# Feed-forward matmuls that stream their moving columns, and write their PSUM columns, last first

## The chip, the core and the metric

The kernel runs on one core of one Trainium2 chip. Its time is the device time of one execution in microseconds (us), the median of three runs. The core has a matrix engine (TensorE; in the profile PE for the matmuls and PEld for the weight loads that run beside them), VectorE (DVE), ScalarE (ACT), GpSimd (POOL) and a queue that issues most DMAs (SyncE, SP). A matmul holds a block of 128x128 weights in the array (the stationary operand), streams the columns of a second operand out of SBUF past it (the moving operand), and writes or adds one column of results into PSUM for every column streamed.

## What is computed

The reference is one inference step over four layers of a diffusion backbone, for 128 context tokens and 256 latent tokens, 1024 wide, all in float32. Every layer is a half-step feed-forward, a token mixer (windowed, global, latent-compressed or neighbourhood attention), and another half-step feed-forward. The change touches the feed-forward alone:

```
def modulate(x, g, shift, scale):
    return rms_norm(x, g) * (1 + scale) + shift
...
def half_ffn(x, shift, scale, gate, g, w_gu, w_down):
    h = modulate(x, g, shift, scale)
    a, u = jnp.split(h @ w_gu, 2, axis=-1)
    return x + FFN_RES * gate * ((jax.nn.silu(a) * u) @ w_down)
```

`w_gu` is 1024 x 5632 and `w_down` 2816 x 1024. There are eight such half-steps.

## The kernel before

Channels lie on the 128 partitions and tokens along the free axis, so the 384 tokens of both sequences are the moving columns of one matmul. A float32 product is made of three matmuls in the type float32r: the operands are split into a high and a low part (`w_hi`, `w_lo`; `h_hi`, `h_lo`; `act_hi`, `act_lo`), and high x high, high x low and low x high are summed in PSUM.

There are twelve stages: stages 0, 2, 3, 5, 6, 8, 9, 11 are feed-forwards, and stages 1, 4, 7, 10 the mixers A, B, C, D. A feed-forward stage on TensorE is:

- `gu_first` (the matmul of line 824): the first 128 columns of gate and of up. For each of 8 input tiles `k` it waits for `h_ready` and issues 6 matmuls, 48 in all. After `k` = 2 and 6 it puts in a few small matmuls for the norm's statistics (banks of their own).
- `gu_step` (lines 840 and 845), 21 times: after the wait for the high weights, for each of gate and up and each `k` one matmul against `h_hi` and one against `h_lo` (32); after the wait for the low weights, 16 more of `w_lo` against `h_hi`. Each has 386 moving columns (`N_MOVE`: 384 tokens and two columns that carry the shift of the modulation), read as `h[:, k, :]`.
- `dn_step` (lines 859 and 863), 8 times: 44 matmuls of `w_hi` against `act_hi` and `act_lo`, then 22 of `w_lo` against `act_hi`, each with 384 moving columns, all added up in one PSUM bank.

That makes 48 + 21 x 48 + 8 x 66 = 1584 matmuls in a stage, 12672 in eight. The moving operand is read in ascending order, one 4-byte element after the other, and the PSUM columns 0 to 385 (or 383) of a bank are written in ascending order. The starts of the moving operands in SBUF are set by padding: `ROOM_HI, ROOM_LO = 24, 56` and `ACT_ROOM = 40` (in elements), and a step of `N_ROW = 448` elements between the tiles `k` of `h`.

The order on every engine is written out by hand and kept by semaphores. Only the last matmul of a step signals (`w_used`). VectorE then reads the bank whole (L1725 and L1726 for gate and up, L1718 for the residual), ScalarE applies SiLU (L1307), and VectorE and ScalarE split the next chunk of weights (L1593, L1263) that SyncE's DMAs bring in. PSUM banks alternate, so that TensorE goes on with the next step meanwhile (waits on `u_ready` and `x_updated` guard a bank's reuse). Beside that VectorE works out the modulation of the next layer from slabs of `mod_w` (L1613).

The mixers' matmuls (projections at L880, output at L1060, scores, transposes) have code of their own.

Of the kernel before, what the change touches and what calls it, by code (L numbers as in the profile page):

```python
# [13 lines left out]
P = 128  # L14
# [4 lines left out]
N_TOK = N_CTX + N_LAT  # L19
TT = N_TOK // P  # L20
N_MOVE = N_TOK + 2
# [3 lines left out]
KF = D_FF // P  # L25
# [49 lines left out]
B_DN = (4, 5)  # L75
# [122 lines left out]
def first_col(x):  # L198


    return P if x == 0 else 0


class Count:
# [49 lines left out]
def build(nc, a, out):  # L254
    with ExitStack() as ctx:
        def sb(name, shape, dt=F32):
            return ctx.enter_context(nc.sbuf_tensor(name, shape, dt))[:]
# [4 lines left out]
        ps = ctx.enter_context(nc.psum_tensor("ps", [P, 8, 512], F32))[:]  # L262
# [6 lines left out]
        w_hi = [sb(f"w_hi{i}", [P, SLOT], F32R) for i in range(2)]  # L269
        w_lo = [sb(f"w_lo{i}", [P, SLOT], F32R) for i in range(2)]  # L270

        def input_of(s):


            at = (ROOM_HI, ROOM_LO) if s % 3 != 1 else (0, 32)
            return [z[:, i:i + KD * N_ROW].rearrange("p (k n) -> p k n", k=KD)[:, :, 0:N_MOVE]
                    for z, i in zip(h_room, at)]
# [165 lines left out]
        for kind in "FABCD":  # L443
            with ExitStack() as own:
# [12 lines left out]
                w = C_UQ_W + C_UKV_W if kind == "C" else QKV_W  # L457
# [73 lines left out]
        act_hi, act_lo = [z[:, ACT_ROOM:ACT_ROOM + KF * N_TOK] for z in tiles["F"]["act"]]  # L531
# [236 lines left out]
        def _(pe):  # L768
# [17 lines left out]
            def stats(s):  # L786

                pe.wait_ge(ssq_ready.sem, ssq_ready.after(s - 1, KD - 1))
                for t in range(TT):
                    mm = pe.matmul(ps[:, B_NORM, t:t + 1], ssq[:, t * P:(t + 1) * P], ones[:, 0:1],  # L790
                                   start=True, stop=True)
                mm.then_inc(stats_made.sem, 1)
# [14 lines left out]
            def broadcast(s):  # L807

                pe.wait_ge(rstd_ready.sem, rstd_ready.after(s))
                for t in range(TT):  # L810
                    mm = pe.transpose(ps[:, B_NORM, t * P:(t + 1) * P], rstd[:, t:t + 1].to_broadcast([P, P]), ident[:])
                mm.then_inc(rbc_made.sem, 1)

            def gu_first(s):


                h_hi, h_lo = input_of(s)
                pe.wait_ge(w_split_lo.sem, w_split_lo.after(s, 0))
                w = [q[0][:, 0:GU_CHUNK].rearrange("p (k u c) -> p k u c", k=KD, u=2) for q in (w_hi, w_lo)]
                for k in range(KD):  # L820
                    pe.wait_ge(h_ready.sem, h_ready.after(s, k))
                    for u in range(2):
                        for i, (lh, rh) in enumerate(((w[0], h_hi), (w[0], h_lo), (w[1], h_hi))):
                            mm = pe.matmul(ps[:, u, 0:N_MOVE], lh[:, k, u, :], rh[:, k, :],  # L824
                                           start=(k == 0 and i == 0), stop=(k == KD - 1 and i == 2))
                    if k == 2:
                        stats(s)
                    if k == 6:
                        broadcast(s)
                mm.then_inc(w_used.sem, 1)  # L830

            def gu_step(s, j, par):
                h_hi, h_lo = input_of(s)
                pe.wait_ge(w_split_hi.sem, w_split_hi.after(s, j))
                pe.wait_ge(u_ready.sem, u_ready.at[s] + j - 1)
                w = [q[par][:, 0:GU_CHUNK].rearrange("p (k u c) -> p k u c", k=KD, u=2) for q in (w_hi, w_lo)]
                for u in range(2):
                    for k in range(KD):
                        for h in (h_hi, h_lo):
                            pe.matmul(ps[:, 2 * par + u, 0:N_MOVE], w[0][:, k, u, :], h[:, k, :],  # L840
                                      start=(k == 0 and h is h_hi), stop=False)
                pe.wait_ge(w_split_lo.sem, w_split_lo.after(s, j))
                for u in range(2):
                    for k in range(KD):
                        mm = pe.matmul(ps[:, 2 * par + u, 0:N_MOVE], w[1][:, k, u, :], h_hi[:, k, :],  # L845
                                       start=False, stop=(k == KD - 1))
                mm.then_inc(w_used.sem, 1)

            def dn_step(s, m, par, first=False):
                c = GU_STEPS + m  # L850
                pe.wait_ge(w_split_hi.sem, w_split_hi.after(s, c))
                pe.wait_ge(x_updated.sem, x_updated.at[s] + m - 1)
                if first:
                    pe.wait_ge(act_ready.sem, act_ready.after(s, KF - 3))
                for k in range(KF):
                    if first and k >= KF - 2:
                        pe.wait_ge(act_ready.sem, act_ready.after(s, k))
                    for y in (act_hi, act_lo):
                        pe.matmul(ps[:, B_DN[par], 0:N_TOK], w_hi[par][:, k * P:(k + 1) * P],  # L859
                                  y[:, k * N_TOK:(k + 1) * N_TOK], start=(k == 0 and y is act_hi), stop=False)  # L860
                pe.wait_ge(w_split_lo.sem, w_split_lo.after(s, c))
                for k in range(KF):
                    mm = pe.matmul(ps[:, B_DN[par], 0:N_TOK], w_lo[par][:, k * P:(k + 1) * P],  # L863
                                   act_hi[:, k * N_TOK:(k + 1) * N_TOK], start=False, stop=(k == KF - 1))
                mm.then_inc(w_used.sem, 1)

            def project(s, g, t, ks):
# [80 lines left out]
            def scores(s, b):  # L948

                kind = stage_kind(s)  # L950
                v = tiles[kind]
                p, x = divmod(b, 2)
                g, at, lat = p // per_pair(kind), first_col(x), 1 + x
                if x == 0:
                    pe.wait_ge(qkt_ready.sem, qkt_ready.after((s, p), len(qkt_types(kind, p)) - 1))
# [43 lines left out]
            def values(s, b, tiles_of):  # L999
# [4 lines left out]
                v = tiles[kind]  # L1004
                p, x = divmod(b, 2)
                g, at, lat = p // per_pair(kind), first_col(x), 1 + x
                pe.wait_ge(pt_ready.sem, pt_ready.after((s, p, x), 1))
                if x == 0 and p >= 1:
# [161 lines left out]
            for s in range(N_STAGE):  # L1170
# [70 lines left out]
                for c in range(WO_STEPS):  # L1241
                    n = n_down[kind] + n_g + c
                    par = n % 2
                    pe.wait_ge(w_split_hi.sem, w_split_hi.after(s, n))
                    pe.wait_ge(w_split_lo.sem, w_split_lo.after(s, n))
                    for b in range(2):
# [3 lines left out]
                        for p in range(PAIRS):  # L1250
                            if p not in begun[m]:
                                mm = output(s, m, p)
# [981 lines left out]
```

## Time and profile before

| | us |
|---|---|
| median of 3 runs | 2933.23 (2933.21 to 2933.38) |
| span of the profiled execution | 2931.5 |
| TensorE matmuls busy | 2900.1 (99%) |
| TensorE weight loads busy | 2810.0 (96%) |
| VectorE busy | 2274.4 (78%) |
| ScalarE busy | 1252.3 (43%) |
| DMA: moved by 16 engines | 490.22 MB, mean 167 GB/s |

The span is from the first to the last instruction; the median of the runs is 1.7 us above it. An instruction of TensorE lasts from its start to the modelled end of its last column. Several matmuls are in flight at a time, so the duration of one is longer than the distance to the next, and "busy" is the time in which at least one is in flight. The rate of the stream is read from the distance between starts.

### The profile page before, as it was taken

What the parts mean: (1) busy time and instruction counts of PE and PEld (TensorE: products, weight loads), DVE (VectorE), ACT (ScalarE), POOL (GpSimd) and SP (SyncE); (2) the same over time, 40 slices, a digit from 0 to 9 for tenths busy, and PEclk for the clock granted to TensorE, in tenths of its full rate; (3) what the DMA queues carried; (4) which work ended last, traced back from release to release, by engine and by line L of the source; (5) the groups of instructions that cost most, each with busy time, mean ns of one, the idle gap of its engine ahead of it and who ended that gap; (6) DMA issues with size and microseconds to landing.
All of it is one profiled execution on the core that took longest, in us unless ns stands there. A gap on an engine that the chain in (4) does not pass through costs nothing.

```text
span 2931.5 us, 44455 instructions
## 1 busy us (share of the span) xinstructions
PE 2900.1 (99%) x17613; PEld 2810.0 (96%) x17613; DVE 2274.4 (78%) x3459; ACT 1252.3 (43%) x2001; POOL 166.6 (6%) x171
## 2 busy tenths in 40 slices
PE   8999999999999999999999999999999999999999
PEld 6999979999999998999999997899999999989999
DVE  6889887888787877888788777778888887777653
ACT  3332464443333266443333348644333333664432
POOL 0000220000000030000000012000000001320000
PEclk9999999999999999999999999999999999999999
DMA  7555314555455512455455531255555555324342
GB/s 290 208 211 216 145 42 170 187 201 204 181 190 190 217 56 93 186 193 210 180 191 199 198 120 46 73 201 193 199 190 192 193 207 195 108 75 173 128 143 93
DMA packets 87722, 490.22 MB, mean 167 GB/s; under 512 B 11824, under 2 KB 13168, under 8 KB 51376
## 3 DMA queue, kind: packets, MB, share of 16 engines
q1 hardware_dynamic: 83696, 480.42, 44.4%
q0 software_dynamic: 3904, 8.24, 1.1%
q8 instruction: 68, 1.11, 0.2%
q14 instruction: 54, 0.44, 0.0%
HBM read 485.33 MB, written 3.29 MB: 167 GB/s over the span
## 4 chain that ended last, share of the span: by engine, by line
PE 55%; issue 38%; DVE 4%; ACT 1%; DMA 1%; POOL 1%; SPq 0%; DVEq 0%; POOLq 0%; ACTq 0%
PE ps L840 16%; PE ps L859 8%; PE ps L845 8%; PE ps L880 5%; PE ps L1060 4%; PE ps L863 4%; PE ps L824 1%; PE ps L995 1%; PE ps L1035 1%; DMA boot<-in_mod_w 1%; PE ps L1134 1%; PE ps L976 1%; PE ps L980 1%; DVE tmp L1685 0%; PE ps L1079 0%
## 5 line engine op out<-in xcount | busy, mean ns | idle before, releaser
L840 PE MATMUL ps<-h_hi,w_hi 128*128 128x386 f32 x2688 | 908.2, 338 | 0.0
L840 PE MATMUL ps<-h_lo,w_hi 128*128 128x386 f32 x2688 | 893.4, 332 | 0.0
L1593 DVE TENSOR_TENSOR w_lo<-w_raw,w_hi 128x2048 fp32r<-128x2048 f32 (+3 forms) x282 | 706.9, 2507 | 30.0 <-ACT w_hi L1263 29.6
L1613 DVE CUSTOM_DVE_ANT_0 F_junk<-F_slab,cond,mod_b 128x1024 f32<-128x1024 f32 x544 | 707.2, 1300 | 12.7
L1263 ACT ACTIVATE w_hi<-w_raw 128x2048 fp32r<-128x2048 f32 (+4 forms) x278 | 578.7, 2082 | 14.8 <-DMA w_raw<-in_ffn_dn 10.8
L840 PEld LDWEIGHTS ps<-h_lo,w_hi 128*128 128x128 f32 x2688 | 512.5, 191 | 0.0
L840 PEld LDWEIGHTS ps<-h_hi,w_hi 128*128 128x128 f32 x2688 | 503.1, 187 | 0.4 <-ACT w_hi L1263 0.4
L845 PE MATMUL ps<-h_hi,w_lo 128*128 128x386 f32 x2688 | 494.4, 335 | 0.0
L859 PE MATMUL ps<-F_act_hi,w_hi 128*128 128x384 f32 x1408 | 473.6, 336 | 0.0
L859 PE MATMUL ps<-F_act_lo,w_hi 128*128 128x384 f32 x1408 | 473.3, 336 | 0.0
L845 PEld LDWEIGHTS ps<-h_hi,w_lo 128*128 128x128 f32 x2688 | 469.0, 187 | 0.0
L1307 ACT ACTIVATE sq<-sq 128x128 f32<-128x128 f32 x176 | 70.8, 403 | 827.1 <-DVE sq L1725 827.0
L1725 DVE TENSOR_TENSOR sq<-ps,rbc 128x386 f32<-128x386 f32 x176 | 98.5, 560 | 254.0 <-PE ps L845 234.1
L1298 ACT ACTIVATE sq<-x 128x384 f32<-128x384 f32 x96 | 50.2, 523 | 571.0 <-DVE x L1718 571.0
L859 PEld LDWEIGHTS ps<-F_act_hi,w_hi 128*128 128x128 f32 x1408 | 264.4, 188 | 0.0
L859 PEld LDWEIGHTS ps<-F_act_lo,w_hi 128*128 128x128 f32 x1408 | 264.3, 188 | 0.0
L863 PE MATMUL ps<-F_act_hi,w_lo 128*128 128x384 f32 x1408 | 254.7, 336 | 0.0
L863 PEld LDWEIGHTS ps<-F_act_hi,w_lo 128*128 128x128 f32 x1408 | 245.2, 188 | 0.0
L1718 DVE SCALAR_TENSOR_TENSOR x<-ps,mod,x 128x128 f32<-128x128 f32 x192 | 71.1, 413 | 137.0 <-PE ps L863 132.3
L1731 DVE SCALAR_TENSOR_TENSOR tmp<-tmp,sq 128x128 f32<-128x128 f32 x352 | 131.1, 414 | 5.7 <-ACT sq L1308 5.7
L880 PE MATMUL ps<-w_hi,h_hi 128*128 128x384 f32 x384 | 133.6, 348 | 0.8 <-DVE h_lo L1692 0.6
L677 POOL TENSOR_TENSOR stats_of<-stats_of,neghalf 128x3 f32<-128x3 f32 x12 | 10.3, 857 | 2173.7 <-DVE stats_of L1654 2173.7
(371 smaller groups left out, 3465.9 us busy)
## 6 DMA issues: line engine op xcount, KB each, us to landing
w_raw<-in_ffn_gu SPq DMA_DIRECT2D x176, 1024.0 KB, 4.8
F_slab<-in_mod_w SPq DMA_DIRECT2D x272, 512.0 KB, 5.6
w_raw<-in_ffn_dn SPq DMA_DIRECT2D x64, 1408.0 KB, 6.4
w_raw<-in_d_w SPq DMA_DIRECT2D x8, 1536.0 KB, 6.7
boot<-in_mod_w SPq DMA_DIRECT2D x8, 1024.0 KB, 10.2
w_raw<-in_a_w SPq DMA_DIRECT2D x4, 1536.0 KB, 6.6
w_raw<-in_b_w SPq DMA_DIRECT2D x4, 1536.0 KB, 6.7
w_raw<-in_c_w SPq DMA_DIRECT2D x8, 544.0 KB, 3.6
```

What stands on the lines that cost most here:

```text
L840: pe.matmul(ps[:, 2 * par + u, 0:N_MOVE], w[0][:, k, u, :], h[:, k, :], start=(k == 0 and h is h_hi), stop=False)
L845: mm = pe.matmul(ps[:, 2 * par + u, 0:N_MOVE], w[1][:, k, u, :], h_hi[:, k, :], start=False, stop=(k == KD - 1))
L859: pe.matmul(ps[:, B_DN[par], 0:N_TOK], w_hi[par][:, k * P:(k + 1) * P], y[:, k * N_TOK:(k + 1) * N_TOK], start=(k == 0 and y is act_hi), s ...
L863: mm = pe.matmul(ps[:, B_DN[par], 0:N_TOK], w_lo[par][:, k * P:(k + 1) * P], act_hi[:, k * N_TOK:(k + 1) * N_TOK], start=False, stop=(k == ...
L880: mm = pe.matmul(ps[:, proj_bank(kind, g, t), 0:QKV_W], x1[:, k, t * P:(t + 1) * P], rh[x2][par][:, k * QKV_W:(k + 1) * QKV_W], start=(k = ...
L1060: mm = pe.matmul(ps[:, wo_bank(m), 0:N_TOK], (w_hi, w_lo)[lh][par][:, cols], o[rh], start=(p == 0 and i == 0), stop=(p == PAIRS - 1 and i ...
L1263: act.activation(w_hi[par][:, 0:w], w_raw[par][:, 0:w], ACT.Copy).then_inc(w_split_hi.sem, 1)
L1593: dve.tensor_tensor(w_lo[par][:, 0:w], w_raw[par][:, 0:w], w_hi[par][:, 0:w], ALU.subtract).then_inc(w_split_lo.sem, 1)
L1613: dve.tensor_tensor_reduce(out=junk[:], in0=w, in1=cond[:, c, :], scale=scale, scalar=mod_b[:, n:n + 1], op0=ALU.mult, op1=ALU.add, accum_ ...
L1718: ins = dve.scalar_tensor_tensor(out=xs, in0=ps[:, bank, i:j], scalar=gate, in1=xs, op0=ALU.mult, op1=ALU.add)
L1725: dve.tensor_tensor(sq[par][:], ps[:, 2 * par, 0:N_MOVE], rbc[:], ALU.mult).then_inc(a_ready.sem, 1)
L1731: ins = dve.scalar_tensor_tensor(out=tmp[par][:, a0:a1], in0=tmp[par][:, a0:a1], scalar=tmp[par][:, N_TOK + c:N_TOK + c + 1], in1=sq[par][ ...
```

## The change

A helper gives an access pattern with its innermost axis turned round: it starts at the last element and has the step negated. It is put around the moving operand and around the PSUM output of each matmul in `gu_first`, `gu_step` and `dn_step`. Since both are turned, column i of the input still ends in column i of the output. The stationary operand is left as it was.

```
+def backward(z):
+
+
+    step, n = z.ap[-1]
+    return bass.AP(tensor=z.tensor, offset=z.offset + (n - 1) * step, ap=[*[list(d) for d in z.ap[:-1]], [-step, n]])
...
-                            mm = pe.matmul(ps[:, u, 0:N_MOVE], lh[:, k, u, :], rh[:, k, :],
+                            mm = pe.matmul(backward(ps[:, u, 0:N_MOVE]), lh[:, k, u, :], backward(rh[:, k, :]),
                                            start=(k == 0 and i == 0), stop=(k == KD - 1 and i == 2))
...
-                            pe.matmul(ps[:, 2 * par + u, 0:N_MOVE], w[0][:, k, u, :], h[:, k, :],
+                            pe.matmul(backward(ps[:, 2 * par + u, 0:N_MOVE]), w[0][:, k, u, :], backward(h[:, k, :]),
                                       start=(k == 0 and h is h_hi), stop=False)
...
-                        mm = pe.matmul(ps[:, 2 * par + u, 0:N_MOVE], w[1][:, k, u, :], h_hi[:, k, :],
+                        mm = pe.matmul(backward(ps[:, 2 * par + u, 0:N_MOVE]), w[1][:, k, u, :], backward(h_hi[:, k, :]),
                                        start=False, stop=(k == KD - 1))
...
-                        pe.matmul(ps[:, B_DN[par], 0:N_TOK], w_hi[par][:, k * P:(k + 1) * P],
-                                  y[:, k * N_TOK:(k + 1) * N_TOK], start=(k == 0 and y is act_hi), stop=False)
+                        pe.matmul(backward(ps[:, B_DN[par], 0:N_TOK]), w_hi[par][:, k * P:(k + 1) * P],
+                                  backward(y[:, k * N_TOK:(k + 1) * N_TOK]), start=(k == 0 and y is act_hi), stop=False)
...
-                    mm = pe.matmul(ps[:, B_DN[par], 0:N_TOK], w_lo[par][:, k * P:(k + 1) * P],
-                                   act_hi[:, k * N_TOK:(k + 1) * N_TOK], start=False, stop=(k == KF - 1))
+                    mm = pe.matmul(backward(ps[:, B_DN[par], 0:N_TOK]), w_lo[par][:, k * P:(k + 1) * P],
+                                   backward(act_hi[:, k * N_TOK:(k + 1) * N_TOK]), start=False, stop=(k == KF - 1))
```

In the built program every engine has the same instructions in the same order, with the same waits, as before; only these matmuls' two access patterns differ (step -1 and the start moved to the last column: 1540 bytes on for 386 columns, 1532 bytes for 384). The helper is seven lines long, so every line below it has a number higher by 7 (line 840 becomes 847).

## Rows read from the trace of the kernel before

**Rows 1.** The page's first two parts: busy us, share, instructions; TensorE's granted clock.

```profile
PE 2900.1 (99%) x17613; PEld 2810.0 (96%) x17613; DVE 2274.4 (78%) x3459; ACT 1252.3 (43%) x2001; POOL 166.6 (6%) x171
...
PEclk9999999999999999999999999999999999999999
```

**Rows 2.** Windows by stage: the feed-forwards; window, length, busy (count) of each engine, clock.

```profile
core 0: us, PE busy (x) PEld busy (x) DVE busy (x) ACT busy (x) POOL busy (x), PEclk, DMA share, GB/s
...
46.40:314.70 268.30, 268.27 (x1545) 267.95 (x1544) 245.46 (x349) 90.16 (x103) 0.00 (x0) 1.00 0.61 221
...
465.50:1017.60 552.10, 552.10 (x3188) 552.03 (x3187) 448.32 (x640) 202.11 (x239) 1.73 (x2) 1.00 0.53 196
...
1162.90:1715.10 552.20, 552.20 (x3188) 552.13 (x3187) 448.42 (x640) 201.50 (x239) 1.73 (x2) 1.00 0.52 195
...
1904.30:2456.40 552.10, 552.10 (x3188) 552.03 (x3187) 448.30 (x640) 201.52 (x239) 1.70 (x2) 1.00 0.52 196
...
2652.10:2931.50 279.40, 276.32 (x1595) 275.97 (x1593) 153.23 (x203) 102.91 (x117) 0.87 (x1) 1.00 0.39 137
```

**Rows 3.** Waits of TensorE, longest in total first: us, times, longest.

```profile
PE ps L1149 <- ACT cond_t L1480: 4.8, 1, 4.8
PE ps L1155 <- DMA boot<-in_mod_w: 4.1, 5, 1.3
PE ps L995 <- DVE A_p L1962: 3.3, 4, 1.3
```

**Rows 4.** Groups by line and shape, TensorE: xcount, busy us, mean ns, idle before.

```profile
L840 PE MATMUL ps<-h_hi,w_hi 128*128 128x386 f32 x2688 | 908.2, 338 | 0.0
L840 PE MATMUL ps<-h_lo,w_hi 128*128 128x386 f32 x2688 | 893.4, 332 | 0.0
L845 PE MATMUL ps<-h_hi,w_lo 128*128 128x386 f32 x2688 | 494.4, 335 | 0.0
L859 PE MATMUL ps<-F_act_hi,w_hi 128*128 128x384 f32 x1408 | 473.6, 336 | 0.0
...
L824 PE MATMUL ps<-h_hi,w_hi 128*128 128x386 f32 x128 | 44.5, 348 | 0.7 <-DVE h_lo L1669 0.7
```

**Rows 5.** Timeline of TensorE, a gate/up step: start us, duration us, instruction.

```profile
600.27 0.34 PE L840 MATMUL ps<-h_hi,w_hi 128*128 128x386 f32 x1
...
600.45 0.33 PE L840 MATMUL ps<-h_lo,w_hi 128*128 128x386 f32 x1
...
600.62 0.34 PE L840 MATMUL ps<-h_hi,w_hi 128*128 128x386 f32 x1
...
605.12 0.34 PE L840 MATMUL ps<-h_hi,w_hi 128*128 128x386 f32 x1
```

**Rows 6.** The same of a down step.

```profile
700.17 0.34 PE L859 MATMUL ps<-F_act_lo,w_hi 128*128 128x384 f32 x1
...
703.29 0.34 PE L859 MATMUL ps<-F_act_lo,w_hi 128*128 128x384 f32 x1
```

**Rows 7.** The same of mixer A's projection, whose moving operand is the weights.

```profile
322.64 0.34 PE L880 MATMUL ps<-w_lo,h_hi 128*128 128x384 f32 x1
...
324.75 0.34 PE L880 MATMUL ps<-w_lo,h_hi 128*128 128x384 f32 x1
```

**Rows 8.** The same at the start: float32 matmuls of 512 columns that fill time.

```profile
12.45 1.13 PE L776 MATMUL ps<-ident,ones 128*128 128x512 f32 x2
...
25.99 2.84 PE L776 MATMUL ps<-ident,ones 128*128 128x512 f32 x6
```

**Rows 9.** Groups by line and shape, VectorE: L1921 reads `D_bias` with step -1, L1853 ascends.

```profile
L1921 DVE TENSOR_TENSOR ps<-ps,D_bias 128x512 f32<-128x512 f32 x16 | 11.1, 695 | 7.3 <-PE ps L983 7.2
...
L1853 DVE TENSOR_TENSOR C_qn<-C_kraw,C_hrs 128x512 f32<-128x512 f32 x8 | 5.5, 694 | 2.1 <-POOL C_hrs L677 1.7 <-DVE C_qraw L1831 0.2
```

## The prediction, made before the changed kernel was run

> **What bounds the kernel now.** I read the page's busy shares first, then the windows by stage, then the waits, and last the timeline inside a step. TensorE is busy for 2900.1 of 2931.5 us, and its clock is granted in full in every slice [rows 1]. The five windows of feed-forwards [rows 2] add up to 268.3 + 552.1 + 552.2 + 552.1 + 279.4 = 2204.1 us, three quarters of the span. In each of them the matmuls are busy from end to end but for the last 3 us of the last one. VectorE, the next busiest, has work for 245.5 of 268.3 us in the first window and for 448 of 552 in the later ones. The longest waits of TensorE in the whole program are 4.8, 4.1 and 3.3 us, in the start-up and in mixer A [rows 3]. The groups of the feed-forward show almost nothing idle ahead of them [rows 4]. So no wait sets the end in these stages. The rate at which matmuls follow one another does.
>
> That rate is the number to watch. In a gate/up step the starts at 600.27 and 605.12 us are 28 matmuls apart [rows 5]: 4.85 / 28 = 173.2 ns for 386 columns. In a down step 700.17 to 703.29 us are 18 matmuls [rows 6]: 3.12 / 18 = 173.3 ns for 384 columns. The clock is at its upper level, 2.4 GHz, so 386 columns at one per tick are 161 ns and 384 are 160. About 12.5 ns are left per matmul. A duration of 332 to 338 ns [rows 4] is therefore nearly two matmuls in flight, not the price of one. The number of matmuls touched is 8 x (48 + 21 x 48) = 8448 of 386 columns and 8 x 8 x 66 = 4224 of 384, together 12672. Times 173.5 ns that is 2199 us, which is the 2204 us of the windows. One nanosecond per matmul is 12.7 us, or 0.43% of the kernel. An effect of half a nanosecond per matmul would be seen, and nothing hides it, since TensorE itself is the bound.
>
> **The change part by part.** *Instructions, waits, DMAs:* none is added, removed or moved on any engine, and no queue has anything else ahead of it. Cost 0.
>
> *Who reads the results:* VectorE waits for the last matmul of a step and then takes the bank whole, so which column is written last matters to nobody. Only the last column of the last matmul counts, and there is one in either order. Cost 0. If it did cost the latency of some columns, that would happen on VectorE, which has slack in these windows [rows 2]; only in the last residual would it be on the path, and below 1 us.
>
> *The moving read in descending order:* no TensorE instruction of this trace does it, so I bound it by the nearest rows. From below there is VectorE's L1921, which reads `D_bias` with step -1: 695 ns for 128x512, against 694 ns for L1853, the same size ascending [rows 9]. Direction costs VectorE 1 ns in 695. But VectorE takes about one element in more than a nanosecond, and TensorE takes one in 0.42 ns. This row shows that addresses can run down, not that they can at TensorE's pace. From above there are the float32 matmuls of L776 [rows 8]: the run of 6 lasts 2.84 us and the run of 2 lasts 1.13, so one more costs (2.84 - 1.13) / 4 = 0.4275 us for 512 columns. That is 0.835 ns per column, two ticks where float32r takes one. If a turned pattern pushed float32r to the pace of two ticks, a matmul of 386 columns would take 12.5 + 386 x 0.835 = 334.8 ns instead of 173.5, 161 ns more, and one of 384 columns 160 ns more: 8448 x 0.161 + 4224 x 0.160 = 2036 us. Between the ends lies L880 [rows 7]: 322.64 to 324.75 us are 12 matmuls, so 175.8 ns each for 384 columns, 2.5 ns more than L859 with as many. These read another tensor at other addresses. So where and how a stream lies in memory is worth some 2.5 ns a matmul, either way: 12672 x 2.5 = 32 us.
>
> *The PSUM write in descending order:* the same two ends, and not a second time. The read and the write go at one pace, so if either needs two ticks per column the matmul does, and if both do it still takes two. A bank starts at an even column and 386 and 384 are even, so columns 385 and 384 are a pair that lies together, as 0 and 1 do before.
>
> *Which value I take:* 0 for both, by the row of VectorE, which is the only one with a descending operand. The tiles, their alignment and the order of matmuls are the same. The trace gives no sign that the rows of the moving operand are limited by their direction, and the start moves by 1540 or 1532 bytes, within 4 bytes of 1536, which is itself the distance between neighbouring `act` tiles that go by at 173 ns [rows 6].
>
> The sum is 0 on the profiled execution's 2931.5 us. With the 1.7 us between span and median it is 2933.2 us.
>
> A rule of the Trainium skill speaks against the change. "PSUM — Partial Sum Buffer" (Specifications) says that PSUM is organised in 8-byte lines, two float32 each, and that any access pattern that isn't contiguous slows matmuls significantly. Read by the letter, a descending pattern isn't contiguous, and the result would be the slow rival below; read by the line, the two halves of each 8 bytes still follow each other, and nothing changes. The Trainium skill's "SBUF — State Buffer" (Specifications) asks for at least two hits per 16-byte line, which a descending read has as an ascending one does. Neither page names a price, and no row of this trace shows TensorE on a descending pattern.
>
> **The rivals.**
>
> *Two ticks per column.* The engine reaches one float32r column per tick only for ascending neighbours, on the read or on the write, and goes to the pace of L776 otherwise. For it: the trace has every float32r stream ascending with step 1, and TensorE does have a pace of two ticks [rows 8]. Against it: VectorE doesn't care [rows 9], and the pairs still lie together. Time: 2933 + 2036 = 4969 us. If the 12.5 ns per matmul vanish under the slower stream, 12672 x 12.5 ns = 158 us come off, 4811 us. Everything else would fit under it, as VectorE's 448 us under more than 1000. This is the case on the other side, and it decides as soon as either the read or the write can't go down at one column per tick.
>
> *A few nanoseconds more per matmul.* The stream starts elsewhere and crosses memory the other way than before, while weights are loaded beside it, and the padding of `h` and `act` was laid out for the ascending start. By L880 a worse position costs 2.5 ns: 2933 + 32 = 2965 us. From 0.5 ns on it would be seen.
>
> *A few nanoseconds less.* The same with the other sign. There are 12.5 ns beyond the columns themselves, and a part may depend on how the streams meet. By the same 2.5 ns: 2933 - 32 = 2901 us. Against both: `h_hi`, `h_lo`, `act_hi` and `act_lo` start at different places, and all average 173 ns [rows 5, 6].
>
> *It doesn't do what it says.* The pattern might be turned back before it reaches the chip. Since the built program holds the step of -1 this has little chance, and it gives the same time as my forecast.
>
> **How the numbers follow.** No change, my forecast: 0.42 (0.02 of it for the last rival). Two ticks per column: 0.26. A few ns more: 0.17. A few ns less: 0.15. The predicted time is that of the likeliest, 2933.2 us, and its own range is 2928 to 2939 us. For the range that should hold 8 in 10 I can't leave out the case of two ticks, so it goes up to 4975 us; downwards it takes in a gain of 2.5 ns per matmul, 2900 us. It holds nearly two clusters with little between: 2900 to 2985 and 4800 to 4975. About 0.2% (6 us, 0.46 ns per matmul) is what a measurement of this kernel tells from no change. Faster by more than that: 0.15. Within it: 0.42. Slower: 0.26 + 0.17 = 0.43. The two slower cases together weigh a hair more than the forecast, but each alone weighs less.
>
> **What the profile would show.** If I am right, the groups of lines 847, 852, 866 and 870 have mean durations of 332 to 338 ns again, their starts in the timeline are 173 ns apart, and the windows of two feed-forwards are 552 us long. With two ticks per column the starts are 335 ns apart, the mean duration is near 500 ns, a window is near 1060 us, VectorE's busy share falls from 78% to under 50%, and the mixers keep their length. With a few ns, the starts are 171 or 176 ns apart at an unchanged pattern of waits. A window that became longer at unchanged distances between starts, with TensorE waiting, would prove the whole argument wrong, since I hold that no wait is touched.

## The result

The change made the kernel slower: 2982.09 us (2981.69 to 2982.45, 4 runs) against 2933.31 us (2933.21 to 2933.52, 4 runs). The ratio is 1.0166, with a 95% interval of 1.0153 to 1.0179. That is 48.8 us more. The span of the profiled execution is 2980.1 us against 2931.5, 48.6 us more.

First the page of the kernel after, which answers [rows 1]: busy us, share and instructions of each engine, then TensorE's granted clock in 40 slices.

```profile
PE 2948.9 (99%) x17613; PEld 2859.8 (96%) x17613; DVE 2273.9 (76%) x3459; ACT 1251.4 (42%) x2001; POOL 166.6 (6%) x171
...
PEclk9999999999999999999999999999999999999999
```

TensorE has the same 17613 matmuls and is busy 48.8 us longer. VectorE and ScalarE do the same work in the same time, and the clock is the same. Next the windows of the kernel after (window, length, busy and count of each engine). The first two hold two feed-forward stages each, the last holds stage 11 and the end. They answer the second, third and fifth of [rows 2], and the fourth is like them.

```profile
471.00:1035.60 564.60, 564.60 (x3189) 564.52 (x3188) 448.22 (x640) 201.97 (x239) 1.73 (x2) 1.00 0.51 192
1180.80:1745.30 564.50, 564.50 (x3189) 564.42 (x3188) 448.15 (x640) 201.38 (x239) 1.73 (x2) 1.00 0.51 191
2694.60:2980.10 285.50, 282.40 (x1595) 282.04 (x1593) 153.12 (x203) 102.87 (x117) 0.87 (x1) 1.00 0.37 134
```

Two stages take 564.6 us in place of 552.1, with as many matmuls and no gap between them. The longest waits of TensorE in the kernel after are still those of the start-up and of mixer A [rows 3]:

```profile
PE ps L1162 <- DMA boot<-in_mod_w: 5.1, 7, 1.5
PE ps L1156 <- DMA ident<-in_ident: 4.9, 1, 4.9
PE ps L1002 <- DVE A_p L1969: 3.3, 4, 1.2
```

So the time is not in a wait. (The second answers the 4.8 us of before; the profile names another releaser for it.) The timeline of a gate/up step (start us, duration us, instruction) shows where it is. The two rows are 28 matmuls apart, as the first and last of [rows 5] are:

```profile
480.63 0.34 PE L847 MATMUL ps<-h_hi,w_hi 128*128 128x386 f32 x1
...
485.62 0.34 PE L847 MATMUL ps<-h_hi,w_hi 128*128 128x386 f32 x1
```

4.99 / 28 = 178.2 ns, against 173.2. In a down step the following rows are 18 matmuls apart, as those of [rows 6] are:

```profile
706.78 0.34 PE L866 MATMUL ps<-F_act_hi,w_hi 128*128 128x384 f32 x1
...
709.96 0.34 PE L866 MATMUL ps<-F_act_hi,w_hi 128*128 128x384 f32 x1
```

3.18 / 18 = 176.7 ns, against 173.3. Averaged over all distances of a stage (1007 between the starts in its 21 gate/up steps, 527 in its down steps), the trace gives 173.55 and 173.76 ns before, and 178.19 and 176.27 after, in every stage (but 174.03 for gate/up of the very first stage before). Such an average is the time from the first start to the last, divided by the number of distances. The groups by line, which answer [rows 4], show it as longer durations at the same count:

```profile
L847 PE MATMUL ps<-h_lo,w_hi 128*128 128x386 f32 x2688 | 915.1, 340 | 0.0
L847 PE MATMUL ps<-h_hi,w_hi 128*128 128x386 f32 x2688 | 914.9, 340 | 0.0
L852 PE MATMUL ps<-h_hi,w_lo 128*128 128x386 f32 x2688 | 505.3, 341 | 0.0
L866 PE MATMUL ps<-F_act_hi,w_hi 128*128 128x384 f32 x1408 | 478.6, 340 | 0.0
```

The sum closes: 8064 matmuls of the gate/up steps x 4.64 ns = 37.4 us, 4224 of the down steps x 2.51 ns = 10.6 us, together 48.0 of 48.6 us. The rest is small and goes both ways: the 384 matmuls of `gu_first` add 1.8 us, while stage 0's gate/up, which was a little slower before, takes 0.5 us off and the work between the stages 0.9. The distances in what follows are given in these two numbers per stage, "gate/up" and "down".

The eight feed-forward stages agree with each other to 0.01 ns (but for gate/up of stage 0), so one kernel can hold a different treatment in each. Most experiments below are built that way: the treatment is a table by stage, and the result is read per stage from the trace. Their line numbers differ a little from those of the change. Where a treatment sends results to the wrong columns or leaves some out, its expectation says so. Apart from the two kernels at the end, each ran once. How far such a reading can be trusted shows in the stages that were left as in one of the two kernels: in every run they gave its distances again within 0.02 ns (but for gate/up of stage 0, which differs by up to 0.5).

### The profile page after: what moved, and what is told of

Its sections match the earlier page's. It is cut to its first block, busy times and chain, and to the rows that moved or that the text cites. A ratio compares the mean times of both kernels' runs of the same rounds, so it can differ in the third digit from the quotient of the medians.

```text
span 2980.1 us, 44455 instructions
## 1 busy us (share of the span) xinstructions
PE 2948.9 (99%) x17613; PEld 2859.8 (96%) x17613; DVE 2273.9 (76%) x3459; ACT 1251.4 (42%) x2001; POOL 166.6 (6%) x171
## 4 chain that ended last, share of the span: by engine, by line
PE 55%; issue 38%; DVE 4%; ACT 1%; DMA 1%; POOL 1%; SPq 0%; DVEq 0%; POOLq 0%; ACTq 0%
PE ps L847 16%; PE ps L866 8%; PE ps L852 8%; PE ps L887 5%; PE ps L1067 4%; PE ps L870 4%; PE ps L831 1%; PE ps L1002 1%; PE ps L1042 1%; PE ps L1141 1%; DMA boot<-in_mod_w 1%; PE ps L983 1%; PE ps L987 1%; DVE tmp L1692 0%; PE ps L1086 0%
## 5 line engine op out<-in xcount | busy, mean ns | idle before, releaser
L847 PE MATMUL ps<-h_lo,w_hi 128*128 128x386 f32 x2688 | 915.1, 340 | 0.0
L1620 DVE CUSTOM_DVE_ANT_0 F_junk<-F_slab,cond,mod_b 128x1024 f32<-128x1024 f32 x544 | 706.3, 1298 | 12.7
L852 PE MATMUL ps<-h_hi,w_lo 128*128 128x386 f32 x2688 | 505.3, 341 | 0.0
L847 PEld LDWEIGHTS ps<-h_lo,w_hi 128*128 128x128 f32 x2688 | 504.9, 188 | 0.0
L852 PEld LDWEIGHTS ps<-h_hi,w_lo 128*128 128x128 f32 x2688 | 479.9, 188 | 0.0
```

What stands on the lines that cost most here:

```text
L847: pe.matmul(backward(ps[:, 2 * par + u, 0:N_MOVE]), w[0][:, k, u, :], backward(h[:, k, :]), start=(k == 0 and h is h_hi), stop=False)
L852: mm = pe.matmul(backward(ps[:, 2 * par + u, 0:N_MOVE]), w[1][:, k, u, :], backward(h_hi[:, k, :]), start=False, stop=(k == KD - 1))
L1620: dve.tensor_tensor_reduce(out=junk[:], in0=w, in1=cond[:, c, :], scale=scale, scalar=mod_b[:, n:n + 1], op0=ALU.mult, op1=ALU.add, accum_ ...
```

## Experiments

### Read or write

```
+READ, WRITE, WTS = {2: True, 5: True, 6: True, 9: True}, {2: True, 5: True, 6: True, 11: True}, {}
...
+def turned(which, s, z):
+
+    return backward(z) if which.get(s, which.get(None, False)) else z
...
-                            pe.matmul(ps[:, 2 * par + u, 0:N_MOVE], w[0][:, k, u, :], h[:, k, :],
+                            pe.matmul(turned(WRITE, s, ps[:, 2 * par + u, 0:N_MOVE]), turned(WTS, s, w[0][:, k, u, :]), turned(READ, s, h[:, k, :]),
```

The lines are those of the difference from the kernel before. `WTS` is empty in every run, so the weights' own order is never turned.

> One kernel, the treatment set per feed-forward stage: stages 0, 3, 8 as before (read and write ascending), 2, 5, 6 as the change (both descending), 9 only the read descending, 11 only the PSUM write descending. Stages 9 and 11 therefore put results of tokens in mirrored columns, which is part of the measurement. Distances between matmul starts, gate/up (386 columns) and down (384): before 173.6 and 173.8 ns, change 178.3 and 176.3 ns. Theory READ (the descending stream out of SBUF costs it): stage 9 shows 178.3 / 176.3, stage 11 shows 173.6 / 173.8. Rival WRITE (the descending order of PSUM columns costs it): stage 11 shows 178.3 / 176.3, stage 9 shows 173.6 / 173.8. Rival BOTH: each shows a part, adding up to +4.6 / +2.5 ns.

The windows of this kernel, TensorE alone: 170 us of gate/up and 90 us of down, in stages 8 (both ascending), 9 (only the read descending) and 11 (only the write descending). The number behind x is how many matmuls the window touches.

```profile
1934.00:2104.00 170.00, 170.00 (x982) 1.00 0.52 193
2108.00:2198.00 90.00, 90.00 (x520) 1.00 0.51 196
2211.00:2381.00 170.00, 170.00 (x956) 1.00 0.49 182
2389.00:2479.00 90.00, 90.00 (x512) 1.00 0.52 200
2688.00:2858.00 170.00, 170.00 (x982) 1.00 0.40 147
2862.00:2952.00 90.00, 90.00 (x520) 1.00 0.32 112
```

Stage 9 fits 956 and 512 matmuls, stages 8 and 11 fit 982 and 520. The averages are 178.19 / 176.27 ns for stage 9 and 173.55 / 173.76 for stage 11. To the hundredth of a nanosecond, the read carries the whole loss and the PSUM write carries none. READ held, and WRITE and BOTH are out, at the places that the operands have in the change. In all runs below read and write are turned together.

### Does the place in SBUF matter?

```
+ROOMS = {0: (24, 56), 2: (23, 55), 3: (22, 54), 5: (21, 53), 6: (20, 52), 8: (16, 48), 9: (8, 40), 11: (0, 32)}
-            at = (ROOM_HI, ROOM_LO) if s % 3 != 1 else (0, 32)
+            at = ROOMS[s] if s % 3 != 1 and s < N_STAGE else (0, 32)
...
+ACT_ROOMS = {0: 40, 2: 41, 3: 42, 5: 43, 6: 44, 8: 48, 9: 56, 11: 64}
```

> Both descending everywhere, as the change, but the place of the moving operands in SBUF shifted per stage: h_hi and h_lo of stages 0, 2, 3, 5, 6, 8, 9, 11 start 0, 1, 2, 3, 4, 8, 16, 24 elements earlier, act_hi and act_lo 0, 1, 2, 3, 4, 8, 16, 32 elements later. Theory POSITION (the padding suited the ascending start, the descending stream meets memory at a worse phase): the distance between starts varies over the stages, and some shift brings gate/up back to 173.6 ns (2 elements, if it is the end of 386 columns in the middle of a 16-byte line; then down, whose 384 columns end on a line, gains nothing from 4). Rival DIRECTION (descending costs it wherever the stream lies): all stages stay near 178.3 and 176.3 ns, within 1 ns.

> Both ascending everywhere, as before, with the same shifts per stage as the descending run. Theory POSITION: ascending streams lose at some of these shifts what the change lost, so some stages show 176 to 178 ns. Rival DIRECTION: all stages stay at 173.6 and 173.8 ns within 1 ns.

In both kernels `act` of stage 11 lies 24 elements later (64 - 40), not 32 as the expectation says. Two further kernels had eight more places for `h` and seven for `act`, since 24 came again:

> More places for the ascending streams: h_hi and h_lo start 5, 6, 7, 9, 12, 15, 20, 22 elements earlier than before in stages 0, 2, 3, 5, 6, 8, 9, 11, act_hi and act_lo 5, 6, 7, 11, 12, 19, 24, 64 later. Theory POSITION: values spread between 172 and 179 ns as in the first run of this kind, and if the pattern repeats every 16 or 32 elements, act +19 is near act +3 (172.2 ns). Against it: all values beyond 8 elements are alike.

> The same places with the moving read and the PSUM write descending. Theory DIRECTION PLUS PLACE (a descending stream has no place as good as the ascending one's): the best stage stays above 175 ns, and the mean over places stays some 2.5 ns above that of the ascending run. Rival PLACE ALONE: some place gives 173.6 ns or less with the descending stream too, and the means over places are the same.

The distances in ns by place (h: elements earlier than before; act: elements later):

| h | 0 | 1 | 2 | 3 | 4 | 5 | 6 | 7 | 8 | 9 | 12 | 15 | 16 | 20 | 22 | 24 |
|---|---|---|---|---|---|---|---|---|---|---|---|---|---|---|---|---|
| ascending | 173.8 | 173.3 | 177.2 | 177.9 | 176.3 | 173.3 | 176.8 | 177.4 | 176.7 | 173.3 | 177.8 | 176.7 | 177.6 | 175.3 | 173.9 | 176.7 |
| descending | 178.2 | 176.7 | 178.5 | 179.0 | 177.8 | 177.4 | 178.9 | 177.8 | 179.2 | 176.8 | 178.8 | 177.8 | 177.8 | 178.1 | 178.9 | 177.8 |

| act | 0 | 1 | 2 | 3 | 4 | 5 | 6 | 7 | 8 | 11 | 12 | 16 | 19 | 24 | 24 | 64 |
|---|---|---|---|---|---|---|---|---|---|---|---|---|---|---|---|---|
| ascending | 173.8 | 178.7 | 177.5 | 172.2 | 175.7 | 178.4 | 175.4 | 172.3 | 174.1 | 173.3 | 174.9 | 173.4 | 173.3 | 173.4 | 173.4 | 173.4 |
| descending | 176.3 | 178.2 | 178.2 | 179.0 | 176.7 | 176.7 | 177.8 | 178.9 | 175.9 | 181.3 | 177.7 | 175.2 | 178.9 | 175.5 | 175.6 | 176.3 |

The place 24 of `act`, measured in two kernels and in different stages, came back within 0.02 ns, so the stage doesn't matter.

In the windows the table reads as follows: the ascending kernel in stages 2 and 8, then the descending one in stages 2 and 8, 170 us of gate/up each.

```profile
477.00:647.00 170.00, 170.00 (x983) 1.00 0.52 192
...
1931.00:2101.00 170.00, 170.00 (x964) 1.00 0.50 186
```

```profile
482.00:652.00 170.00, 170.00 (x964) 1.00 0.50 185
...
1949.00:2119.00 170.00, 170.00 (x951) 1.00 0.49 180
```

Both causes are there. One element of place is worth up to 5.3 ns per matmul (act, ascending: 177.5 at 2, 172.2 at 3). So DIRECTION in its pure form is out. But the descending stream is the slower one at 29 of the 31 places (not at act 1 and 5), on average by 2.2 ns for h (178.1 against 175.9) and by 2.9 ns for act (177.5 against 174.6), and none of its 16 places for h comes below 176.7 ns. The difference at one place runs from -1.7 to +8.0 ns, so the averages are rough. Still, no descending place comes near 173.6 ns (the best is 175.15), so PLACE ALONE is out as well, and DIRECTION PLUS PLACE held. By these averages half of the 4.6 ns of h is the lost place: the kernel before, at 173.6, stands 2.3 ns below the mean of its places, and the change, at 178.2, stands on the mean of the descending ones. In down both stand a little below their means, and the whole 2.5 ns is the direction. This split is a reckoning from averages; no run takes the two apart. The two elements that were to line up the end of the 386 columns with a 16-byte line did nothing (178.5). Nor does the ascending pattern simply repeat after 16 elements: act 19 is at 173.3 where act 3 is at 172.2. From 11 elements on, the ascending values of `act` in this table are alike but for 12 (173.3 to 173.4, and 174.9), while those of `h` spread from 173.3 to 177.8.

### The place relative to what?

```
+W_SHIFT = {0: 0, 2: 1, 3: 2, 5: 3, 6: 4, 8: 8, 9: 16, 11: 24}
...
+def beside(s, z):
+
+    return bass.AP(tensor=z.tensor, offset=z.offset + W_SHIFT[s], ap=[list(d) for d in z.ap])
...
-                            pe.matmul(ps[:, 2 * par + u, 0:N_MOVE], w[0][:, k, u, :], h[:, k, :],
+                            pe.matmul(turned(WRITE, s, ps[:, 2 * par + u, 0:N_MOVE]), beside(s, w[0][:, k, u, :]), turned(READ, s, h[:, k, :]),
```

> Moving read and PSUM write ascending, moving operands where they are before. Only TensorE's view of the weights is shifted, per stage: stages 0, 2, 3, 5, 6, 8, 9, 11 load weights 0, 1, 2, 3, 4, 8, 16, 24 elements further on in the same tile (so they multiply by the wrong channels, which is part of the measurement). Theory MEETING (the moving stream and the weight load of the next matmul get in each other's way, by their distance in memory): shifting the weights up by n is the same as shifting h down by n, so gate/up repeats the ascending run with shifted h: 173.6, 173.3, 177.2, 177.9, 176.3, 176.7, 177.6, 176.7 ns. Rival OWN PLACE (a moving stream has a cost by its own address alone): all stages stay at 173.6 ns for gate/up and 173.8 for down.

> The same shifts of TensorE's view of the weights with the moving read and the PSUM write descending as in the change. Theory MEETING: gate/up repeats the descending run with shifted h: 178.2, 176.7, 178.5, 179.0, 177.8, 179.2, 177.8, 177.8 ns in stages 0, 2, 3, 5, 6, 8, 9, 11. Rival OWN PLACE: 178.2 ns for gate/up and 176.3 for down in every stage.

Distances of gate/up in ns:

| weights later / h earlier by | 1 | 2 | 3 | 4 | 8 | 16 | 24 |
|---|---|---|---|---|---|---|---|
| ascending, weights shifted | 176.1 | 177.1 | 178.2 | 176.7 | 176.66 | 177.62 | 176.71 |
| ascending, h shifted | 173.3 | 177.2 | 177.9 | 176.3 | 176.67 | 177.63 | 176.73 |
| descending, weights shifted | 177.9 | 178.3 | 178.3 | 179.4 | 179.17 | 177.78 | 177.78 |
| descending, h shifted | 176.7 | 178.5 | 179.0 | 177.8 | 179.16 | 177.78 | 177.78 |

Windows of 170 us of gate/up in stage 8 with the weights shifted by 8, first ascending and then descending:

```profile
1932.00:2102.00 170.00, 170.00 (x965) 1.00 0.50 186
```

```profile
1947.00:2117.00 170.00, 170.00 (x950) 1.00 0.49 181
```

OWN PLACE is out: h lay where it lies before, and its stream became up to 4.6 ns slower. For shifts of 8, 16 and 24 elements, MEETING holds to 0.02 ns in either direction: there only the distance between the moving operand and the weights counts. For 1 to 4 elements it holds roughly at best (ascending 1: 176.1 against 173.3, descending 4: 179.4 against 177.8), so at small shifts something else counts beside the distance. In down the shifted weights gave 174.4 to 175.6 ns ascending (173.8 unshifted) and 175.2 to 177.2 descending (176.3), so OWN PLACE is out there too. MEETING is not tested in down, because `act` was moved only the other way.

### Fewer weight columns

```
+W_COLS = {0: 128, 2: 128, 3: 64, 5: 64, 6: 32, 8: 32, 9: 96, 11: 96}
...
+def cols(s, last):
+
+    return P if last else W_COLS[s]
...
+                        mm = pe.matmul(turned(WRITE, s, ps[0:cols(s, k == KD - 1), 2 * par + u, 0:N_MOVE]), w[1][:, k, u, 0:cols(s, k == KD - 1)], turned(READ, s, h_hi[:, k, :]),
```

> Only the low-weight runs of matmuls (w_lo against h_hi or act_hi, 16 in a gate/up step, 22 in a down step) are changed: all but the last of each bank load fewer weight columns, 64 in stages 3 and 5, 32 in 6 and 8, 96 in 9 and 11; 128 in 0 and 2. Ascending in stages 0, 3, 6, 9, descending in 2, 5, 8, 11. The correction by w_lo is left out for the other output channels. With 128 columns the distances in these runs are 173.9 and 173.5 ns ascending, 177.7 and 175.6 descending. Theory MEETING (the weight load beside the stream is what costs): the time above the 161 ns of the columns shrinks with the columns loaded, to under half of it at 64 and to 1 to 4 ns at 32, and ascending and descending come within 1 ns of each other. Rival FIXED (a cost of starting any stream, and a descending one more): the distances stay at 173 to 174 and 175 to 178 ns whatever is loaded.

The weight loads of this line, all stages together (count, busy us, mean ns, idle before), show that the loads did become shorter:

```profile
L868 PEld LDWEIGHTS ps<-h_hi,w_lo 128*128 128x128 f32 x924 | 166.3, 188 | 10.5
L868 PEld LDWEIGHTS ps<-h_hi,w_lo 128*96 128x96 f32 x588 | 95.1, 162 | 8.0
L868 PEld LDWEIGHTS ps<-h_hi,w_lo 128*64 128x64 f32 x588 | 79.6, 135 | 21.0
L868 PEld LDWEIGHTS ps<-h_hi,w_lo 128*32 128x32 f32 x588 | 64.1, 109 | 33.8
```

From 188 to 109 ns over 96 columns is 0.82 ns per column. The distances between two matmuls with such loads, without the first distance of each bank, are:

| weight columns | 128 | 96 | 64 | 32 |
|---|---|---|---|---|
| gate/up ascending | 173.7 | 176.8 | 175.7 | 173.8 |
| gate/up descending | 178.1 | 179.9 | 178.4 | 178.7 |
| down ascending | 173.3 | 173.6 | 175.0 | 173.5 |
| down descending | 175.5 | 176.6 | 175.5 | 179.2 |

No narrower load made the distance shorter, and several made it longer, by up to 3.6 ns. The expectation of MEETING, that the loss would shrink with the load and the two directions meet within 1 ns, failed: at 32 columns gate/up is 13 and 18 ns above its columns. FIXED did not hold either, since the distances left its 173 to 174 and 175 to 178 ns. So it isn't how long the load runs beside the stream that costs. Why its width moves the distances at all, and unevenly, stays open.

### Shorter streams

```
+N_COLS = {0: 352, 2: 352, 3: 320, 5: 320, 6: 256, 8: 256, 9: 288, 11: 288}
...
+def some(s, last, z):
+
+    return z if last else z[:, 0:N_COLS[s]]
```

In the second kernel the slice is `z[:, z.shape[1] - N_COLS[s]:z.shape[1]]`, and the third has 382, 380, 376 and 368 columns.

> Only the low-weight runs (w_lo against h_hi or act_hi) are changed: all but the last matmul of each bank stream fewer moving columns, 352 in stages 0 and 2, 320 in 3 and 5, 256 in 6 and 8, 288 in 9 and 11, with all 128 weight columns loaded. The correction by w_lo is left out for the other tokens. Ascending in stages 0, 3, 6, 9, descending in 2, 5, 8, 11. With all columns the distances are 173.9 and 173.5 ns ascending (gate/up, down), 177.7 and 175.6 descending. Theory PER MATMUL (something at the change from one stream to the next): distance = columns / 2.4 + 12.5 ns ascending at 320 and more, and the descending one 2 to 4 ns above it at every length. Rival PER COLUMN (stalls spread over the stream): the part above columns / 2.4 shrinks in proportion, at 256 columns to 8 ns ascending, and the descending surplus to 1.4 to 2.6 ns.

> As the run with shortened low-weight streams (352 columns in stages 0 and 2, 320 in 3 and 5, 256 in 6 and 8, 288 in 9 and 11; ascending in 0, 3, 6, 9, descending in 2, 5, 8, 11), but the last columns of the range are taken and not the first, so that a descending stream starts at the same element as in the change. The correction by w_lo is left out for the other tokens. There, with the first columns, no surplus of the descending streams was left: 159.6 to 160.2 ns at 352 in either direction. Theory START PLACE: it is the place of the first element that matters, so the descending streams show their surplus again, 2 to 4 ns above columns / 2.4 + 13.3, at each length. Rival LENGTH: below 384 columns the load of weights has slack and nothing is to be paid, so all descending streams stay within 1 ns of columns / 2.4 + 13.3 ns as before.

> Low-weight streams shortened by little, the first columns taken: 382 columns in stages 0 and 2, 380 in 3 and 5, 376 in 6 and 8, 368 in 9 and 11, same directions and same omission. Time above columns / 2.4 was 12.8 (gate/up, 386) and 13.3 ns (down, 384) ascending, 16.8 and 15.5 descending, and 12.9 to 13.5 for both at 352. Theory START PLACE: the descending surplus jumps up and down from length to length, since each length moves the first element of the descending stream and not that of the ascending one, which stays at 13 ns. Rival LENGTH: the surplus falls steadily from 382 to 352 columns.

The low-weight run of a gate/up step in the timeline (start us, us for the 16 matmuls together) with 352 columns: ascending in stage 0 and descending in stage 2 with the first columns, then descending in stage 2 with the last columns.

```profile
102.81 2.76 PE L868 MATMUL ps<-h_hi,w_lo 128*128 128x352 f32 x16
```

```profile
494.31 2.76 PE L868 MATMUL ps<-h_hi,w_lo 128*128 128x352 f32 x16
```

```profile
494.55 2.85 PE L868 MATMUL ps<-h_hi,w_lo 128*128 128x352 f32 x16
```

Time above columns / 2.4 in ns, between two shortened matmuls and without the first distance of each bank ("all": the same matmuls in the kernels before and after):

| columns | 256 | 288 | 320 | 352 | 368 | 376 | 380 | 382 | all |
|---|---|---|---|---|---|---|---|---|---|
| gate/up ascending, first columns | 11.0 | 13.1 | 14.3 | 13.5 | 13.4 | 15.0 | 15.8 | 15.8 | 12.8 |
| gate/up descending, first columns | 11.2 | 11.9 | 13.2 | 12.9 | 15.2 | 18.3 | 15.2 | 16.5 | 17.3 |
| gate/up ascending, last columns | 12.8 | 12.6 | 14.5 | 13.5 | | | | | |
| gate/up descending, last columns | 13.8 | 16.5 | 16.5 | 19.5 | | | | | |
| down ascending, first columns | 11.5 | 13.4 | 13.5 | 13.4 | 15.5 | 16.6 | 15.4 | 14.2 | 13.3 |
| down descending, first columns | 11.1 | 11.1 | 13.3 | 13.3 | 13.8 | 16.4 | 15.3 | 17.6 | 15.5 |
| down ascending, last columns | 11.5 | 11.7 | 13.5 | 15.6 | | | | | |
| down descending, last columns | 11.1 | 11.3 | 13.3 | 13.3 | | | | | |

In the first kernel the descending surplus was gone from 352 columns down, against both PER MATMUL and PER COLUMN. In the second it was back in gate/up (19.5 ns at 352, 16.5 at 320 and 288, but only 1 ns above the ascending one at 256), where the streams start at the same element as in the change. So a shorter stream doesn't cure it by itself, and LENGTH fails there. In down, with the same start as in the change, it stayed away, so START PLACE fails there. There it was the ascending stream of 352 that became slower (15.6 ns). In the third kernel neither direction is steady from 368 to 382 columns: it is neither the steady fall of LENGTH nor an ascending stream that stays at 13 ns. What all of them have in common is that no stream paid less than 11 ns beyond its columns: the least is 11.0 and 11.1 ns at 256 and 288 columns and 13.2 and 12.9 at 320 and 352, and with narrower weights 12.9. From 352 columns down a descending stream can be as cheap as an ascending one. Where exactly the 2 to 6 ns on top arise stays open.

### Places chosen from the sweeps

> Ascending, correct order, places chosen from the earlier runs: h_hi and h_lo start (1, 5), (9, 5), (5, 1), (5, 9), (1, 9), (13, 13), (17, 17), (21, 21) elements earlier in stages 0, 2, 3, 5, 6, 8, 9, 11; act_hi and act_lo (3, 7), (7, 3), (3, 0), (0, 3), (3, 15), (15, 15), (35, 35), (67, 67) later. Theory LINE (an ascending stream that starts on the last element before a multiple of 4 always pays least): all of gate/up at 172 to 173.4 ns and all of down but the two with a 0 at 172.2 to 173.4. Rival CHANCE: the new pairs spread from 173 to 178 ns as the other places did.

The pairs (1, 5), (9, 5), (5, 1), (5, 9), (1, 9), (13, 13), (17, 17), (21, 21) for h gave 175.8, 173.5, 176.0, 175.8, 175.0, 172.6, 178.1 and 175.8 ns. Those for act gave 175.3, 173.4, 174.9, 174.5, 172.2, 172.6, 173.9 and 172.2. LINE is refuted by 178.1 at h 17, which starts in the same place of a line as h 1, 5 and 9. The spread is nearer to CHANCE, but 13 is the best place for h so far. The pairs show one thing more. With both tiles at 1, at 5 or at 9 it was 173.3 ns each time; mixed as (1, 5), (5, 1), (5, 9) and (1, 9) the same places gave 175.0 to 176.0. So the places of `h_hi` and `h_lo` count together.

```
-ROOM_HI, ROOM_LO = 24, 56
-ACT_ROOM = 40
+ROOM_HI, ROOM_LO = 11, 43
+ACT_ROOM = 43
```

That is the ascending kernel (its `READ` and `WRITE` are empty). The descending one has 23, 55 and 56 in these places.

> Reading and writing ascending as before the change; only the places of the moving operands differ: h_hi and h_lo start 13 elements earlier (11 and 43 in place of 24 and 56), act_hi and act_lo 3 later (43 in place of 40). From the sweeps gate/up goes from 173.55 to 172.6 ns and down from 173.76 to 172.2: 8448 x 0.96 + 4224 x 1.54 ns = 14.6 us less than before, 2918.7 us. If place were an artefact of the stage it was measured in, it stays at 2933 us.

> The change (both descending) with the places that suited the descending stream best in the sweeps: h_hi and h_lo 1 element earlier (23 and 55), act_hi and act_lo 16 later (56). Gate/up 176.7 in place of 178.2 ns, down 175.15 in place of 176.3: 8448 x 1.5 + 4224 x 1.1 ns = 17.5 us less than the change, 2964.6 us. If the whole loss of the change were a place that no longer fits, a good place would bring it back to 2933 us.

The ascending kernel took 2919.71 us (5 runs) against 2933.61 (9 runs): ratio 0.9953, interval 0.9940 to 0.9967. It is faster than both kernels, by 13.9 us, where 14.6 were worked out. The descending one took 2964.84 us (4 runs): ratio 1.0107, interval 1.0092 to 1.0122, where 2964.6 were worked out. The windows of stage 2 (gate/up and down), ascending and then descending:

```profile
476.00:646.00 170.00, 170.00 (x987) 1.00 0.52 193
649.00:739.00 90.00, 90.00 (x524) 1.00 0.51 196
```

```profile
480.00:650.00 170.00, 170.00 (x964) 1.00 0.50 186
657.00:747.00 90.00, 90.00 (x516) 1.00 0.51 195
```

The averages are 172.59 / 172.24 ns and 176.67 / 175.15. What was read from single stages adds up over the whole kernel. And the best place found takes the change back by 17.3 us of 48.8, not by all of it. Read at the best places known to each, the two directions are 45.1 us apart. That is nearly the whole 48.8, but the comparison favours the ascending one, for which eight more pairs of places were tried.

## Why the prediction was wrong

**What bounds the kernel now** was right, and so was the scale: one nanosecond per matmul is 12.7 us, and nothing hides it. 3.85 ns per matmul came back as 48.8 us. The "about 12.5 ns" left per matmul is 12.4 in gate/up and 13.3 in down by its own rows, which changes nothing here.

**The parts that cost nothing** cost nothing. No instruction or wait moved (the counts and the three longest waits answer each other, within 1 us), and the columns written last delayed nobody. The PSUM write in descending order is free, as taken, and now measured for itself. Read by the letter, the rule of the Trainium skill that was weighed ("PSUM — Partial Sum Buffer", Specifications) would have made it slow, and the trace doesn't agree: with only the write turned round, the distances stay at 173.55 and 173.76 ns.

**The step that failed** is "Which value I take: 0 for both", for the read. It rested on two readings. The first was the row of VectorE [rows 9]. That engine takes an element every 1.36 ns, and I had said myself that it can't speak for TensorE's pace, but then used it as the value. The second was the sentence that the start moves by about 1536 bytes, a distance between neighbouring `act` tiles, and is therefore the same place. It looks at the first element alone. What the runs showed in place of the 0: with only the read turned round, each matmul takes 4.64 ns more in gate/up and 2.51 in down, which is the whole loss. One element of place is worth up to 5.3 ns, and at equal places the direction still costs 2.2 to 2.9 ns on average. "The trace gives no sign that the rows of the moving operand are limited by their direction" was an absence of evidence: no row of before had a descending operand on TensorE.

**The rivals.** "A few nanoseconds more per matmul" is what happened, with the mechanism as written there (the stream starts elsewhere and crosses memory the other way, beside the weight load, and the padding was laid out for the ascending start). It had a chance of 0.17. Its term was mis-sized: 2.5 ns, from L880 [rows 7], against 4.64 measured in gate/up and 2.51 in down, so 32 us against 48.8. L880 showed one place of another stream, and the places reach over 6.5 ns; that its 2.5 ns is the value measured in down is chance. "Against both: `h_hi`, `h_lo`, `act_hi` and `act_lo` start at different places, and all average 173 ns" was read the wrong way round. That four starts agree doesn't mean that the start is without effect: 12 of the 16 places measured for h ascending are slower. Whether the padding had been tuned isn't shown by any run, but it lies among the better places. Two ticks per column did not happen: a descending stream costs 1.4 to 2.7% of a matmul, not 90%. What the profile would show in this case was named as "171 or 176 ns apart at an unchanged pattern of waits"; it was 178 and 176.

**The chances** put the two slower cases a hair above the forecast, and the measured sign was on that side. The forecast stayed with the single likeliest case, whose support was the weakest inference in the text. The measured time lies inside the range of 2900 to 4975 us, and 3 us inside the end of its lower cluster, but that says little for the argument: the range was drawn so wide for a case that did not happen.

What stays open: why the descending read costs more. In gate/up it follows the distance between the moving operand and the weights for shifts of 8, 16 and 24 elements, it doesn't follow the duration of the load, and neither the first element nor the length explains it alone. Whether the order in which the weights themselves are read has a part in it was not measured, and the write was turned alone at one place only.

## What to carry to other kernels

On a kernel in which matmuls follow each other without a gap, the distance between their starts is the number to read, and in this kernel it depends on where and in which direction the moving operand is streamed: sweep the offset of the moving tensors against the weights by single elements, one place per stage of a single kernel, before and after anything that shifts an allocation. Keep the moving read ascending; the order of the PSUM write cost nothing here. And an operand's behaviour on one engine is no evidence for another that reads three times as fast.

## What the runs showed that was not expected

- The place of a moving operand, in steps of one 4-byte element, moves a float32r matmul of 384 columns from 172.2 to 178.7 ns ascending, and from 175.2 to 181.3 descending. With 386 columns it is 172.6 to 178.1 ascending, and 176.7 to 179.2 descending.
- In gate/up, shifting the weights up by 8, 16 or 24 elements gives the same distance, to 0.02 ns, as shifting the moving operand down by as much.
- A descending PSUM write costs nothing at the places of the kernel before; a descending moving read alone gives the change's distances to 0.01 ns.
- Beyond its columns, a stream of 352 in down pays 13.4 ns ascending and 13.3 descending (160.1 and 160.0 ns), and a stream of 384 or 386 pays 12.2 and 11.8 at the best places found. The Trainium skill's "TensorE: Matmul & The Clock Gate" (Wait — 56ns, not 53.3ns?) gives columns / 2.4 + 2.5 ns for back-to-back matmuls, an estimate of 162.5 ns for 384 columns. These float32r streams, with a weight load ahead of each matmul, measure 172.2 ns at best, so for them the figure is too low.
- A load of 32 weight columns in place of 128 takes 109 ns in place of 188, and doesn't shorten the distance between matmuls of 386 columns (173.8 against 173.7 ns ascending).
